# Two transformer blocks on one core: the places of TensorE's operands in SBUF, modulo 512 bytes

## What is computed

```python
# first block, l = 0 (conv mixer), l = 1 (differential attention); SEQ 256, D 1024, F 2816
h = rms_norm(x, norm_g[l, 0]) * (1 + sc_m) + sh_m        # sc, sh, g: c_act @ mod_w[l] + mod_b[l]
y = conformer_conv(h, ...) if l == 0 else diff_attention(h, k, v, w_q, ...)
x = x + g_m * rms_norm(y, norm_g[l, 1])
h = rms_norm(x, norm_g[l, 2]) * (1 + sc_f) + sh_f
y = conv_ffn(h, ffn_w_in[l], ...)                        # D -> 2F, conv of width 3, silu(g) * v, F -> D
x = x + g_f * rms_norm(y, norm_g[l, 3])
# second block, i = 0 (RWKV-7 time mix), i = 1 (spatial gating)
h = _rwkv7_time_mix(...) if i == 0 else _sgu_mixer(...)
x = x + _rmsnorm(h, norm_gains[i, 1])
x = x + _rmsnorm(_swiglu(_rmsnorm(x, norm_gains[i, 2]), w_gate, w_up, w_down), norm_gains[i, 3])
```

## The kernel before

| operand | place | distance past the weights |
|---|---|---|
| `raw`, `hi`, `lo` | 256 | 0 |
| `OH`, `OL`, `RH2`, `RL2` | 448 | 192 |
| `GH`, `GL` | 448 | 192 |
| `PH`, `PL` | 448 | 192 |

## Time and profile before

### The profile page before, as it was taken

One profiled execution on the slowest core, in us unless ns is written; L12 is line 12 of the kernel. 1 busy time (PEld: TensorE's weight loads), 2 busy tenths in 40 slices (PEclk: granted clock), 3 DMA queues, 4 the chain that ended last, 5 costly groups with the idle time before them and its releaser, 6 DMA issues.

```text
span 1426.0 us, 31047 instructions
## 1 busy us (share of the span) xinstructions
PE 1378.5 (97%) x11806; PEld 1309.1 (92%) x11806; DVE 1047.9 (73%) x1636; ACT 734.9 (52%) x1193; POOL 217.6 (15%) x232
## 2 busy tenths in 40 slices
PE   8999999999988999999999999999999999999997
PEld 6998899999986899999888888799999998999997
DVE  6988799987996788883687965677774556677743
ACT  4547565645357556664366542553444447544442
POOL 0000133310000113321000010123330000133300
PEclk9999999999999999999999999999999999999999
DMA  9874367797881436665432400346666443466662
GB/s 376 304 254 174 123 224 238 258 388 261 312 305 48 162 119 192 191 223 189 162 104 74 120 17 2 101 136 188 184 208 202 146 119 119 139 201 194 211 203 70
DMA packets 68431, 258.16 MB, mean 181 GB/s; under 512 B 7545, under 2 KB 9857, under 8 KB 67970
## 3 DMA queue, kind: packets, MB, share of 16 engines
q1 hardware_dynamic: 68354, 257.10, 54.1%
HBM read 256.01 MB, written 1.06 MB: 180 GB/s over the span
## 4 chain that ended last, share of the span: by engine, by line
PE 80%; DVE 14%; ACT 3%; issue 2%; DMA 1%; DVEq 0%; ACTq 0%
PE ps L725 20%; PE ps L727 20%; PE ps L726 20%; DVE lo L1817 3%; PE ps L742 3%; DVE modraw L1823 2%; PE ps L686 2%; PE ps L688 1%; PE ps L687 1%; ACT hi L1297 1%; DMA modraw<-in_wmod 1%; DVE U L2378 1%; DVE products L2376 1%; PE ps L749 1%; DVE Y L1876 1%
## 5 line engine op out<-in xcount | busy, mean ns | idle before, releaser
L1817 DVE TENSOR_TENSOR lo<-raw,hi 128x1024 fp32r<-128x1024 f32 (+1 forms) x350 | 475.6, 1375 | 172.0 <-ACT hi L1297 171.4
L725 PE MATMUL ps<-OH,lo 128*128 128x256 f32 x1984 | 557.5, 281 | 4.5 <-DVE lo L1817 4.1
L726 PE MATMUL ps<-OL,hi 128*128 128x256 f32 x1984 | 551.8, 278 | 0.0
L727 PE MATMUL ps<-OH,hi 128*128 128x256 f32 x1984 | 551.8, 278 | 0.0
L1297 ACT ACTIVATE hi<-raw 128x1024 fp32r<-128x1024 f32 (+1 forms) x350 | 380.7, 1112 | 15.5 <-DMA raw<-in_w 9.3
L725 PEld LDWEIGHTS ps<-OH,lo 128*128 128x128 f32 x1984 | 373.8, 188 | 10.4 <-DVE lo L1817 7.7
L726 PEld LDWEIGHTS ps<-OL,hi 128*128 128x128 f32 x1984 | 374.2, 189 | 0.0
L727 PEld LDWEIGHTS ps<-OH,hi 128*128 128x128 f32 x1984 | 372.7, 188 | 0.0
L727 PE MATMUL ps<-GH,hi 128*128 128x256 f32 x704 | 196.1, 279 | 0.0
L725 PE MATMUL ps<-GH,lo 128*128 128x256 f32 x704 | 196.1, 278 | 0.0
L726 PE MATMUL ps<-GL,hi 128*128 128x256 f32 x704 | 196.1, 278 | 0.0
(11 more groups left out here) (382 smaller groups left out, 1951.2 us busy)
## 6 DMA issues: line engine op xcount, KB each, us to landing
raw<-in_w SPq DMA_DIRECT2D x288, 512.0 KB, 3.8
raw<-in_w SPq DMA_DIRECT2D x64, 704.0 KB, 5.0
modraw<-in_wmod SPq DMA_DIRECT2D x77, 512.0 KB, 5.5
modlate<-in_wmod SPq DMA_DIRECT2D x6, 512.0 KB, 5.0
modlast<-in_wmod SPq DMA_DIRECT2D x5, 512.0 KB, 4.8
modfirst_a<-in_wmod SPq DMA_DIRECT2D x4, 512.0 KB, 11.5
modfirst_b<-in_wmod SPq DMA_DIRECT2D x4, 512.0 KB, 12.0
l<-in_lora_in SPq DMA_DIRECT2D x1, 1536.0 KB, 6.3
```

The costliest lines, as they stand in the source:

```text
L725: pe.matmul(bank[:, 0:T], lo[:, r, w], oh[:, k0 + k], start=first, stop=False)
L726: pe.matmul(bank[:, 0:T], hi[:, r, w], ol[:, k0 + k], start=False, stop=False)
L727: ins = pe.matmul(bank[:, 0:T], hi[:, r, w], oh[:, k0 + k], start=False, stop=final)
L1817: dve.tensor_tensor(lo[:, s, 0:kt * P], raw[:, s, 0:kt * P], hi[:, s, 0:kt * P].bitcast(F32), ALU.subtract).then_inc(lo_made, 1)
```

## The change

Three small tensors move from behind `xt` to ahead of `raw`, where they take 128 + 32 + 32 = 192 bytes. All that lies between is 192 bytes further up; the arena stays where it was. `GH`, `GL` and `modraw` move up by 256 bytes inside it, `PH` and `PL` by 128. No instruction is added, taken away or moved on any engine: only addresses are other ones.

```diff
         small = fixed("small", [P, 32])
+        ngain = fixed("ngain", [P, 4, DC])
+        dec = fixed("dec", [P, DC])
+        bgain = fixed("bgain", [P, DC])
         raw = fixed("raw", [P, SLOTS, UW])
...
         mods = fixed("mods", [P, 96])
-        ngain = fixed("ngain", [P, 4, DC])
         rgain = fixed("rgain", [P, 4, DC])
...
-        dec = fixed("dec", [P, DC])
         products = fixed("products", [P, 256])
-        bgain = fixed("bgain", [P, DC])
...
-        GH = at(5, "GH", [P, FC, T], F32R, plus=PHASE)
-        GL = at(5, "GL", [P, FC, T], F32R, plus=PHASE + 4 * FC * T)
-        modraw = at(5, "modraw", [P, SLOTS, D], plus=PHASE + 8 * FC * T)
+        GH = at(5, "GH", [P, FC, T], F32R, plus=3 * PHASE)
+        GL = at(5, "GL", [P, FC, T], F32R, plus=3 * PHASE + 4 * FC * T)
+        modraw = at(5, "modraw", [P, SLOTS, D], plus=3 * PHASE + 8 * FC * T)
...
-        PH = at(5, "PH", [P, DC, T], F32R, plus=PHASE)
-        PL = at(5, "PL", [P, DC, T], F32R, plus=PHASE + OPERAND)
+        PH = at(5, "PH", [P, DC, T], F32R, plus=2 * PHASE)
+        PL = at(5, "PL", [P, DC, T], F32R, plus=2 * PHASE + OPERAND)
```

## The result

| | before | after |
|---|---|---|
| median, us | 1435.66 (4 executions) | 1464.53 (4 executions) |
| lowest, highest | 1435.25, 1444.43 | 1461.25, 1467.0 |
| the profiled execution, its time | 1427.87 | 1461.25 |
| its span | 1426.0 | 1459.3 |
| granted clock | 0.995 | 0.997 |

The changed kernel is slower: ratio 1.0172, 95% interval 1.0133 to 1.0212; the two medians alone give 1.0201. Executions more than 1.5% above the fastest of their kernel are left out of all ratios of this document, two of 2269 and 3158 us beside experiment 8 among them, and the upper end of the kernel before's own spread with them. The clock is not the reason for the difference: it stands at its upper level, 2.4 GHz, in both.

The account below looks back on a forecast made before the run. PE, busy 97% of the span, was taken to bound the kernel through its 9024 matmuls. The profiled 1427.87 us, plus 7.9 for redrawn rhythms and 0 to 0.9 for `PH`, gave 1436 us, range 1406 to 1458.

Parts of the forecast that it names:

- What bounds the kernel: PE, busy 97% of the span: the end is set by how fast it goes through its 9024 matmuls.
- two rhythms: PE's main matmuls on `OH` and `GH` go at 113.3 ns (short) or 117.8 ns (long); 4970 short, 4050 long.
- the draw differs between executions of one program: Timed executions have one or two more long feed-forward runs in the 117.8 ns rhythm than the profiled one, 6.8 us each.
- both survive at the new distances: Condition of the 1436 us forecast, chance 0.38: 113.3 and 117.8 ns steps both remain, the slower one's share about half.
- the run at L635: Nine matmuls with operands 128 apart instead of 192: uneven steps, 118 ns each, read as an effect of distance.
- the long one: L725 to L727 on `OH` all at 117.8 ns: 1445 us, with `GH` 1450, at 119.5 ns 1465; chance 0.34.
- 119.5 ns is as far as I stretch it: Upper bound of a matmul step at the new distances: 37 us more, 1465 us.
- If `GL,hi` and `OL,hi` part company, the distance decides: Sign to look for: one mean duration at 276 ns, the other at 281, would mean 0 and 256 differ.
- The terms put at 0: DVE and ACT on `raw`, `hi`, `lo`, POOL on `GH`, `GL`, and small tensors: 0 us; DMA into `raw`: 0, at most 5.
- The rule that nothing happens: PE's independent reading ports make distance cost nothing: 1428 to 1444 us; chance 0.15, counted within the forecast's.

Follow-up runs that it names:

- experiment 8: Kernel before plus two extra 96-column matmuls once in each of the four long runs: 1425.44 us, ratio 0.9962.
- experiments 1 to 4: Changed kernel with distance put back: ratio 1.0023. Kernel before with `GH` 448, `PH` 320: 1.0007; `OH` 256 or 320: 1.0142 or 1.0065; only `GH` 256: 1.0083.
- experiments 1, 3 and 4: Changed kernel with distance put back: 1442.07 us. Kernel before with `OH` at 256: 1458.03, at 320: 1445.92; with only `GH` at 256: 1444.73.
- experiment 6: Kernel before with `lo` 64 bytes further, 128 below the operands, `hi` still 192 from `OH` and `OL`: 1450.46 us, ratio 1.0088.
- table in 5: Steps found at each distance; its own runs, against the kernel before: `OH` at 224, 1451.57 us; `OH` at 352, 1461.14; `OL` alone at 448, 1438.63.
- 7: Four extra 96-column matmuls once in each of the four long runs: kernel before 1426.66 us, ratio 0.9965; changed kernel 1466.42 us, ratio 1.0238.

## Why the prediction was wrong

The forecast was 1436 us with a range of 1406 to 1458; 1464.53 lies above it.

- **What bounds the kernel** held: PE's step times 9024. So did the reading of two rhythms at the same places and clock, and "the draw differs between executions of one program": 22 executions of the kernel before spread over 1420 to 1444 us on one chip, and breaks that set the rhythm cut that to 5 us in one kernel and 9 in the other.
- **The step that failed** is "both survive at the new distances". At 0 and 256, where 8832 of the 9024 matmuls went, neither survives; there is one rhythm, of 120.0 ns. At 128 there are two again, of 118.5 and 120.0 ns, on `PH` alone. It should have been given the largest chance only if a row at another distance had shown 113 ns, and the prediction itself noted that none did. The row that had the right sign was the run at L635, but it could not give a price: I read it as 118 ns for distance 128. In the changed kernel the same run, whose own distance is 128 in both, takes 1.075 us for its 9 steps, 119.4 ns each, against 118.1 before, with steps of 115 to 122 ns against 113 to 124. So nine matmuls do not show a distance's own step; what goes before them counts too.
- **The rival that came true** is the long one, with its place and its sign; the term that was mis-sized is its upper step. "119.5 ns is as far as I stretch it" was short by 0.5 ns, and the range was cut at 118.7, 1.3 ns short. At 9024 matmuls each half nanosecond is 4.5 us. Its price at 119.5 ns, 1465 us, is nearly the measured time by luck, for two errors offset: the step was 120.0, and about 8 us came back, mostly as shorter breaks, a term that the sum did not have at all.
- **"If `GL,hi` and `OL,hi` part company, the distance decides"**: they did not, both went to 283, because 0 and 256 act alike. The distance decides all the same, as experiments 1 to 4 show; that sign was not one that could have told it.
- **The terms put at 0** held in the changed kernel: L1817 1371 ns against 1375, L1297 1110 against 1112, L2608 812 against 813, ACT's waits in all before L1297 15.0 us against 15.5. The plain fp32 sums stayed at 386 ns.
- **The rule that nothing happens.** The Trainium skill, page "SBUF — State Buffer", section "Who interferes with whom", calls PE's two reading ports independent and says "PE and ACT never wait on anyone". By it the distance was to cost nothing, and the trace does not agree: 113.3 to 120.0 ns a step, with nothing changed but addresses (experiments 1, 3 and 4). No run shows whether the ports themselves are where the time goes.

**What stays open.** Why the step depends on the distance was not found. Whether the weights of the next matmul or those of the present one count is not separated (experiment 6). 416 was not tried, and nothing finer than 32 bytes. At 32, 128, 160 and 320 more than one step was seen, so a step seen once at a distance may not be its only one; 32 and 160 on `RH2` rest on 192 matmuls each. Why one kind of break turns the rhythm and another sets it to short is open too.

## What to carry to other kernels

Where PE streams matmuls whose weights change every time, treat the place of the moving operand relative to the weights as a size to be tuned: sweep it in steps of 32 or 64 bytes on the chip, and read the step (window + one duration, divided by the count) of long stretches, not the time alone. When a profile holds the same instructions at two speeds, look at what broke the stream before each; two or more matmuls into a bank that nobody reads, put in at a fixed point, can set the quick one. Try their form on the chip: here two of 96 columns were followed by the quick rhythm each time, and two of 128 columns turned it into the slow one 27 times. Expect breaks to give back a part of what a longer step costs, here 8 of 41 us.

## What the runs showed that was not expected

- The step of a 128x256 fp32r matmul with new weights takes one of some seven values, 113.3 to 120.0 ns, by the distance of its operands; some distances have two of them (table in 5).
- At 192 and 448 the stream has two states. Each holds for up to 1000 matmuls. A break of two or four matmuls of 96 columns left it short each time; the break at L749 changed it each time, in both directions (7). It also turns by itself, in either direction: behind a hitch of some 60 ns, and without one (7, 8).
- One program's time varies by 1.7% between executions (1420.02 to 1444.23 us) without any difference in clock, and four executions don't show it: the four that stood beside the changed kernel lay within 9.2 us.
